# Half 1 of the scale summed on VectorE alone, and expert gate/up products ordered hi x hi, lo rows, lo weights

## The reference

```python
c_act = jax.nn.silu(c)
mod = (c_act @ ada_w[l] + ada_b[l])[:, None, :]
sh1, sc1, g1, sh2, sc2, g2 = jnp.split(mod, 6, axis=-1)
u = _rmsnorm(h, norm1_g[l]) * (1 + sc1) + sh1
h = h + g1 * _mixer(u, ...)            # recurrent and linear-attention branches, w_in is 1024 x 7184
u = _rmsnorm(h, norm2_g[l]) * (1 + sc2) + sh2
h = h + g2 * _moe(u, ...)              # 128 experts, top 8 of each token, plus a shared expert
# one expert: g, up = split(x @ w_gu); (silu(g) * up) @ w_down, with w_gu 1024 x 512, w_down 256 x 1024
```

## Time and profile before

| | |
|---|---|
| time, median of 3 runs | 1391.85 us (1389.2, 1391.85, 1395.33) |
| the profiled execution's own time | 1393.11 us |
| its span, first to last instruction | 1391.3 us |
| mean granted TensorE clock | 0.984 |
| PE busy | 1348.0 us, 97% |
| DVE busy | 839.7 us, 60% |
| ACT busy | 643.7 us, 46% |
| POOL busy | 195.6 us, 14% |
| HBM read and written | 259 GB/s over the span |

### The profile page before, as it was taken

The page is one execution under the profiler, slowest core; times in us unless marked ns, Lnnn a source line. Parts: engine busy times, 40 slices in busy tenths (PEclk is TensorE's granted clock), DMA queues, the critical chain, the costliest instruction groups (busy, mean ns, idle before and its releaser), DMA issues.

```text
span 1391.3 us, 26375 instructions
## 1 busy us (share of the span) xinstructions
PE 1348.0 (97%) x5956; PEld 998.8 (72%) x5957; DVE 839.7 (60%) x1365; ACT 643.7 (46%) x815; POOL 195.6 (14%) x328
## 2 busy tenths in 40 slices
PE   6999999999999999899999999999999999999985
PEld 6778877878888787466777767777667677776742
DVE  4342464965636877577764767767675664455427
ACT  4471246364223313356654656656565554453411
POOL 1000000000000000322222222222222222222200
PEclk9799999999999999999999999999999999999998
DMA  9432111232726752579977879979797866676276
GB/s 329 132 105 77 61 61 61 87 124 93 257 77 236 260 169 93 200 229 319 343 271 243 286 235 342 362 269 344 272 342 258 309 237 230 216 263 227 71 293 282
DMA packets 104720, 301.35 MB, mean 217 GB/s; under 512 B 20540, under 2 KB 23844, under 8 KB 95720
## 3 DMA queue, kind: packets, MB, share of 16 engines
q1 hardware_dynamic: 78808, 258.20, 53.5%
q0 software_dynamic: 20800, 33.61, 7.0%
q10 hardware_dynamic: 5072, 9.02, 1.8%
HBM read 319.61 MB, written 40.90 MB: 259 GB/s over the span
## 4 chain that ended last, share of the span: by engine, by line
PE 89%; DVE 3%; DMA 3%; ACT 1%; issue 1%; SPq 1%; DVEq 0%; ACTq 0%
PE psum L1553 30%; PE psum L1780 26%; PE psum L1822 16%; PE psum L1770 4%; PE psum L1526 2%; PE psum L1709 2%; DMA gu_raw<-in_exp_w_gu 2%; PE psum L1813 2%; PE psum L1846 1%; PE psum L1837 1%; PE psum L1664 1%; DMA w_dn<-in_shared_w_gu 1%; PE psum L1586 1%; DMA ring<-in_ada_w 1%; PE psum L1624 1%
## 5 line engine op out<-in xcount | busy, mean ns | idle before, releaser
L1417 DVE TENSOR_TENSOR gu_lo<-gu_raw,gu_hi 128x1024 f32 x204 | 241.2, 1222 | 92.6 <-ACT gu_hi L946 76.8
L946 ACT ACTIVATE gu_hi<-gu_raw 128x1024 f32 x204 | 211.5, 1056 | 114.1 <-issue 67.0
L1822 PE MATMUL psum<-w_dn,mask 128*128 x560 | 251.6, 592 | 0.0
L1780 PE MATMUL psum<-gu_hi,xT_hi 128*128 (+1 forms) x568 | 228.4, 402 | 1.4 <-DVE gu_lo L1417 1.4
L1780 PE MATMUL psum<-gu_hi,xT_lo 128*128 (+1 forms) x568 | 222.1, 391 | 0.0
L1780 PE MATMUL psum<-gu_lo,xT_hi 128*128 (+1 forms) x568 | 221.0, 389 | 0.0
L1822 PEld LDWEIGHTS psum<-w_dn,mask 128*128 128x128 f32 x560 | 105.9, 189 | 106.1 <-issue 100.6
L446 DVE TENSOR_TENSOR w_lo<-ring,w_hi 128x1024 fp32r<-128x1024 f32 x80 | 94.8, 1222 | 90.2 <-ACT w_hi L439 88.2
L1553 PE MATMUL psum<-uT_hi,w_hi 128*128 128x512 f32 x352 | 139.3, 396 | 1.1 <-DVE w_lo L446 1.1
L439 ACT ACTIVATE w_hi<-ring 128x1024 fp32r<-128x1024 f32 x80 | 82.7, 1056 | 119.4 <-PE psum L1553 58.4
L1553 PE MATMUL psum<-uT_hi,w_lo 128*128 128x512 f32 x352 | 137.1, 389 | 0.0
(11 more groups left out here) (309 smaller groups left out, 1943.7 us busy)
## 6 DMA issues: line engine op xcount, KB each, us to landing
gu_raw<-in_exp_w_gu SPq DMA_DIRECT2D x208, 512.0 KB
w_dn<-in_exp_w_down SPq DMA_DIRECT2D x70, 1024.0 KB
ring<-in_w_in SPq DMA_DIRECT2D x56, 512.0 KB, 5.0
ring<-in_ada_w SPq DMA_DIRECT2D x32, 512.0 KB, 4.9
ring<-expert_rows SPq DMA_DIRECT2D x8, 1024.0 KB, 13.0
ring<-in_ada_w SPq DMA_DIRECT2D x4, 1024.0 KB, 13.3
scale_w<-in_ada_w SPq DMA_DIRECT2D x4, 1024.0 KB, 14.6
ring<-in_w_branch_b SPq DMA_DIRECT2D x8, 512.0 KB, 6.4
```

What stands on the lines that cost most here:

```text
L946: act.activation(gu_of(gu_hi, order, p), gu_raw[:, PK * p:PK * p + PK], ACT.Copy).then_inc(gu_hi_ready, 1)
L1417: tt(gu_of(gu_lo, order, p), gu_raw[:, PK * p:PK * p + PK], gu_of(gu_hi, order, p).bitcast(F32), ALU.subtract).then_inc(gu_split, 1)
L1780: mm = pe.matmul(moe_bank(GU), rows[:, s % 2, k], w[:, bass.ds(order % 2, 1), k].rearrange("p o n -> p (o n)"), start=(k == 0 and m == 0), ...
L1822: mm = pe.matmul(moe_bank(Y0 + g), hT[:, j], w_dn[:, bass.ds(order % 3, 1), j, g * NC:(g + 1) * NC].rearrange("p o n -> p (o n)"), start=( ...
```

## The change

Start: VectorE sums all eight k of the scale's half 1 (`sum_rows` is called a second time, for k = 4 to 7, behind `scale_cols(0)`), PE treats that half as the others (`columns`), ScalarE makes the unrounded rows of k = 0 to 5 and VectorE those of 6 and 7, and VectorE's subtraction of the low-rank weights goes ahead of `scale_cols(1)`. Expert products: `gate_up` takes all 8 k of hi x hi, then all of xT_lo x gu_hi, then all of xT_hi x gu_lo; it waits at its head for xT_hi_ready and gu_hi_ready alone, for xT_ready ahead of the 9th matmul and for gu_split ahead of the 17th.

```diff
-        ACT_FULL = (0, 1, 3, 5)
+        ACT_FULL = (0, 1, 2, 3, 4, 5)
...
-                    if k < ks[-1]:
+                    if k < KT - 1:
                         own(ins)
                     else:
                         ins.then_inc(row_sum, 1)
...
                 if k in ACT_FULL:
-                    dve.wait_ge(u_full, ACT_FULL.index(k) + 1)
+                    dve.wait_ge(u_full, k + 1)
...
             scale_cols(0)
-
-            def full(k):
-                wait_emptied(dve, ("xT", k))
-                own(ts(full_of(k), xnT[:, k], mod_cols[:, KT + k:KT + k + 1], mod_cols[:, k:k + 1], ALU.mult, ALU.add))
-                own.settle()
-
-            full(2)
+            sum_rows(scale_w[:, 1], scale_in[1], tmpT[:, 1], range(4, KT))
             for k in range(4):
                 u_lo(k)
-            scale_cols(1)
-            for k in (4, 6, 7):
-                full(k)
             dve.wait_ge(lr_split, 1)
             dve.wait_ge(lr_zero, 1)
             tt(wlr_lo[:, :, :, 0:RANK], wlr_four, wlr_hi[:, :, :, 0:RANK].bitcast(F32), ALU.subtract).then_inc(lr_split, 1)
+            scale_cols(1)
+            for k in (6, 7):
+                wait_emptied(dve, ("xT", k))
+                own(ts(full_of(k), xnT[:, k], mod_cols[:, KT + k:KT + k + 1], mod_cols[:, k:k + 1], ALU.mult, ALU.add))
+            own.settle()
...
             columns(("scale", 0), 2, tmpT[:, 0])
-            start_job(("scale", 1))
-            pe.matmul(bank(("scale", 1))[:, 0:4], ident[:], zeros[:, 0:4], start=True, stop=False)
-            pe.wait_ge(scale_in[1][1], 16)
-            for k in range(4, KT):
-                for j in range(4):
-                    pe.matmul(bank(("scale", 1))[:, j:j + 1], scale_w[:, 1, k, j * P:(j + 1) * P], c_col[:, k:k + 1], start=False, stop=False)
-            pe.wait_ge(row_sum, 3)
-            for j in range(4):
-                mm = pe.matmul(bank(("scale", 1))[:, j:j + 1], tmpT[:, 1, j * P:(j + 1) * P], ones[:, 0:1], start=False, stop=(j == 3))
-            end_job(mm)
+            columns(("scale", 1), 3, tmpT[:, 1])
...
-            def gate_up(n, s, order, ks=range(KT)):
-
-                if ks[0] == 0:
-                    pe.wait_ge(xT_ready, n + 1)
-                    pe.wait_ge(gu_split, order * PIECES + 2 * PIECES)
-                for k in ks:
-                    for m, (w, rows) in enumerate(((gu_hi, xT_hi), (gu_lo, xT_hi), (gu_hi, xT_lo))):
+            def gate_up(n, s, order):
+
+                pe.wait_ge(xT_hi_ready, n + 1)
+                pe.wait_ge(gu_hi_ready, order * PIECES + PIECES)
+                for m, (w, rows) in enumerate(((gu_hi, xT_hi), (gu_hi, xT_lo), (gu_lo, xT_hi))):
+                    if m == 1:
+                        pe.wait_ge(xT_ready, n + 1)
+                    elif m == 2:
+                        pe.wait_ge(gu_split, order * PIECES + 2 * PIECES)
+                    for k in range(KT):
                         mm = pe.matmul(moe_bank(GU), rows[:, s % 2, k], w[:, bass.ds(order % 2, 1), k].rearrange("p o n -> p (o n)"),
                                        start=(k == 0 and m == 0), stop=(k == KT - 1 and m == 2))
-                if ks[-1] == KT - 1:
-                    mm.then_inc(gu_done, 1)
+                mm.then_inc(gu_done, 1)
```

## The result

| | before | after |
|---|---|---|
| time, median of 5 runs each | 1391.38 us (1388.82 to 1395.33) | 1381.81 us (1381.08 to 1384.3) |
| the profiled execution's own time | 1393.11 us | 1381.24 us |
| its span | 1391.3 us | 1379.5 us |
| mean granted clock | 0.984 | 0.988 |

The medians differ by 9.6 us and the means by 9.2; the ratio is given as 0.9928 (95% interval 0.9913 to 0.9942), which is 10.0 us. The forecast had 7.4 less than the profiled execution and 6.2 less than the median. Runs of both kernels were repeated beside the experiments. Over all of them 74 runs of before have the mean 1390.85 us (standard deviation 2.1) and 23 runs of the change 1382.36 (2.0), so the change is worth **8.5 us, give or take 0.9** (95%, from these two deviations). This is the number that the explanation has to meet; single profiled executions differ by more than what is in dispute.

What follows compares the result with a forecast made beforehand. PE (TensorE), busy 1348.0 of 1391.3 us, was taken to bound the kernel. Start -4.2 and expert loop -3.2 gave -7.4 from the profiled 1393.11, so 1385.7 us; range 1382 to 1390.

Steps and rivals of the forecast that it cites:

- The start, -4.2: Low-rank product (L1624) on PE: starts at 43.5 instead of 47.72, 4.2 us sooner.
- Its chain: Start: VectorE's sums, PE's columns, ScalarE's rows, then the low-rank subtraction ending at 43.5 releases L1624; no new wait.
- The loop, -3.2: Expert products over 68 steps: 3.5 us of waits go, 0.3 returns, gain 3.2 us.
- rival 3: Expert products: two waits inside each break the overlap of matmuls, 22.7 us slower, 1408.4; chance 0.05.
- Rivals 1 and 4: Loop gives nothing, 1388.9, chance 0.18; or something else holds L1624 and only the loop's 3.2 come, 1389.9, chance 0.05.
- against the profiled execution's 1393.11: Base of the sum: -7.4 us taken from the one profiled execution's 1393.11, giving 1385.7.
- 0.3 us of wait returns: Expert loop: PE reaches the transposes of gated row h sooner than its 0.99 us of slack allows, 0.3 us lost.
- the 8.15 us of now: Low-rank product: its 24 matmuls assumed to take 8.15 us as before, between bounds of 5.5 and 10.2.
- rival 2: Clock in the low-rank product: sooner high, 2.7 us less, 1383.0, chance 0.08; low throughout, 1387.7, chance 0.08.
- either bound: Low-rank product's 24 matmuls: all at the low clock 2.0 us more than now, all at the high 2.7 less.

Runs made afterwards that it cites:

- e1: The change with the expert products' old order and waits, so the start's edit alone: mean of 12 runs 1386.60 us, ratio 0.997 to the kernel before.
- e2: The kernel before with the expert products' edit alone, start as before: mean of 12 runs 1387.56 us, ratio 0.9978 to the kernel before.
- e7: The change, but expert products wait at their head for xT_lo and all of gu_lo: mean of 12 runs 1385.79 us, ratio 0.9966 to before.
- e4: The kernel before, unedited, run and profiled a second time: 1390.61 us in one execution.
- e13: The change plus 68 empty PE instructions in three pauses at the start (44, 12, 12): mean 1383.51 us (5 runs, without the profiled one).
- e3: The change itself, unedited, run and profiled again: mean of 6 runs 1382.59 us, 8.3 us below the runs of before beside it.
- e12: The change itself, unedited, run again as partner of other kernels: mean 1381.64 us without the profiled execution.

## Why the prediction was wrong, step by step

**Where it held.** The start, -4.2: -4.3 at the head of the low-rank product, -4.7 at the first w_in product, -4.3 by e1. Its chain was right to 0.2 us, with the low-rank subtraction as the last release and no new wait behind it. The loop, -3.2: -3.3 by e2, -3.4 by e7. Waits inside a product cost nothing; rival 3 is refuted by twelve executions with 10.23 us a step. The Trainium skill (TensorE: Matmul & The Clock Gate, section "Step-by-step: what each phase is for") has only a matmul that stands alone pay for its drain; behind a met wait this one doesn't stand alone, by the 0.23 between starts. Rivals 1 and 4 (nothing from the loop, nothing from the start) are refuted by e2 and e1.

**Where it failed.** The forecast of 1385.7 was 3.9 over the measured median and 3.3 over the mean of all 23 runs.
- The step "**against the profiled execution's 1393.11**" is the larger part. It was known to lie 1.3 over the median, and the forecast kept it as the base anyway. 74 runs put before at 1390.85, so 2.3 us of the 3.3 are this base. Its clock had fallen early at the start: e4, where it fell late, reached the first w_in product 2.35 us sooner (53.52 for 55.87) and took 1390.61. 1390.85 - 7.4 = 1383.5 would have been in the range, 1.1 over the mean.
- The term "**0.3 us of wait returns**" didn't come. With the 3.8 us that the loop carries on average instead of 3.5, the loop gives 0.6 more than forecast, and the start 0.5 (4.7 for 4.2). That makes up the 1.1, though each of the three numbers is uncertain by as much. The start's 0.5 is mostly the product's own time, taken as "**the 8.15 us of now**": on average it is 8.0 us in the four executions with the old start and 7.6 in the eight with the new one.
- The clock was treated as a matter of L1624's own matmuls (rival 2). Those differed little, 8.15 us before, 7.51 after. It varied ahead of the edit. The Trainium skill (same page, section "What's actually happening") says that the number of matmuls at the low clock varies between runs. The traces now agree: 7.0 to 8.4 us for the same 24 in the four profiled executions of the change. That is far from rival 2's 2.7 us less. The larger effect was ahead of them: between these four the product starts at 40.59 to 43.70 and the first w_in product at 48.10 to 51.74, a spread of 3.6 us, more than either bound that the prediction took from L1624 alone.
- Nothing was priced for PE's program getting shorter. That it moved a fetch, shortened a wait by 1.7 us and the routing stage by 2.55 is shown in the profiled executions; that it moved the time of the others isn't.
- The range ended at 1382, 0.2 us over the median that came: its lower end took no account of a base that was too high. The mean of all 23 runs, 1382.36, lies just inside it, so which side of the end the five runs fell on was chance; that the forecast was 3.3 us too high wasn't.

**What stays open:** whether the 8.5 of the whole exceed the 7.6 of the halves at all, what of the routing stage's 2.55 us an execution that isn't profiled keeps, why the clock falls behind the late load in seven executions and not in e13's, and what makes it fall at the start.

## What to carry to other kernels

A forecast of less than 1% needs a base of many runs: take terms from the profiled execution, but subtract them from the mean, and ask what that one execution had of bad luck (here the clock ahead of the edit). Look first at the queue of the engine that releases the bounding one: a subtraction of 0.7 us that stood behind work for later was worth 1.4 us at the head of the product that waited for it, and together with two rows given to an idler engine 3.1 of the start's 4.3 us, while 16 products taken off PE added the rest. A wait belongs ahead of the first matmul that reads the data, and the order should put those matmuls last; in this loop, waits that were already met cost nothing (10.227 us a step with them inside).

## What was not expected of the hardware

- Instruction fetches of PE are DMA packets of 16 KB on the same engines as the data. One in the first 10 us of a 2 MB load goes with a landing at 12.0 to 12.6 us instead of 10.6 to 11.2, and an edit of the program's length moves it.
- Empty PE instructions that count a semaphore cost about 0.15 us each: 12 of them in e13 made a pause of 0.60 us one of 2.38. At the head 68 put the first matmul from 8.3 to 11.4 us, and 44 didn't move it. Batches of 47 between products cost more than batches of 17, which showed nothing.
- The granted clock falls between 28.9 and 32.3 us by execution, for the same program, in the one-column matmuls or the column sums behind them. In e3 and e12, where these matmuls start alike (27.02 and 27.03), this moves the low-rank product by 2.7 us (40.65 and 43.35).
